# A two-block transformer layer on one core: first loads on one queue, one more product behind each modulation sum, attention outputs a slab earlier, the convolution's sums as single products

## The reference

```python
def first_block(x, ...):
    xn = rms_norm(x, norm1_g)
    (sg_u, sg_v, g_q, g_k, g_v, g_r, g_a, a_q, a_k, a_v, c_a, c_g) = split(xn @ w_in)
    y_a = spatial_gating(gelu(sg_u), gelu(sg_v), ...)        # layer norm over sg_v first
    y_b = gated_linear_attention(g_q, g_k, g_v, g_r, g_a, ...)
    y_c = band_chunk_attention(a_q, a_k, a_v, rel_bias)      # softmax(q k^T + bias) v, 8 heads of 64
    y_d = conformer_conv(c_a, c_g, ...)                      # depthwise conv, 31 taps, then layer norm
    merged = sum(sigmoid(xn @ w_gate[n] + b_gate[n]) * (y @ w_branch[n]) for n, y in ...)
    h = x + merged @ w_out
    h = h + square(relu(rms_norm(h) @ w_ff1)) @ w_ff2
    h = h + sigmoid(rms_norm(h) @ w_ple_gate + b) * (p @ w_ple)
    return rms_norm(h)

def second_block(x, c, ...):
    mod = silu(c) @ ada_w + ada_b                            # six vectors of 1,024: the modulation
    h = modulate(rms_norm(x), sh1, sc1)
    mq, mk, mv, mo, mi, mf, aq, ak, av, ga, gb = split(h @ w_in + b_in)
    ym = mlstm(...)                                          # 4 heads of 128
    ya = attention(rope(aq), rope(ak), av)                   # causal here, 8 heads of 64
    merged = sigmoid(ga) * (ym @ p_mlstm) + sigmoid(gb) * (ya @ p_moba)
    x = x + g1 * (merged @ w_out)
    h = modulate(rms_norm(x), sh2, sc2)
    x = x + g2 * ((silu(h @ w_gate) * (h @ w_up)) @ w_down)
    return rms_norm(x)
```

## Time and profile before

| what | before |
|---|---|
| three runs | 918.73, 921.71 and 918.3 us; median 918.73 |
| profiled execution | 917.34 us, of it 916.0 us span |
| PE busy | 897.2 us (98% of the span), 7,348 matmul records |
| DVE busy | 729.7 us (80%) |
| ACT busy | 569.7 us (62%) |
| GpSimd busy | 1.9 us |
| share of the chain that ended last | PE 86%, DVE 7%, ACT 4%, DMA 1%, issue 1% |
| DMA | 189.83 MB, mean 207 GB/s |

### The profile page before, as it was taken

How to read it: one execution, slowest core, us unless ns; L and a number is a source line. 1 busy time by engine, 2 the same in 40 slices (tenths; PEclk the granted TensorE clock), 3 DMA queues, 4 the chain that set the end, 5 groups by cost and what they waited for, 6 DMA issues and landing times.

```text
span 916.0 us, 18439 instructions
## 1 busy us (share of the span) xinstructions
PE 897.2 (98%) x7348; PEld 870.9 (95%) x7348; DVE 729.7 (80%) x1150; ACT 569.7 (62%) x828; POOL 1.9 (0%) x9
## 2 busy tenths in 40 slices
PE   8999999999999999999999989999999999999996
PEld 7999989999999999999999989988999999999996
DVE  5778998889997899888875989987789885555554
ACT  6848456676576687654445777667695664544542
POOL 0000000000000000000000000000000000000000
PEclk9999999999999999999999999999999999999998
DMA  8766546455875689988856546653536656666541
GB/s 302 250 189 220 156 142 202 156 169 194 290 252 176 226 306 341 346 315 306 326 167 202 183 155 201 208 165 119 173 123 197 188 171 201 189 194 197 186 160 47
DMA packets 53157, 189.83 MB, mean 207 GB/s; under 512 B 6208, under 2 KB 6736, under 8 KB 52944
## 3 DMA queue, kind: packets, MB, share of 16 engines
q1 hardware_dynamic: 52496, 187.60, 62.1%
q10 hardware_dynamic: 576, 1.05, 0.3%
HBM read 186.53 MB, written 1.05 MB: 205 GB/s over the span
## 4 chain that ended last, share of the span: by engine, by line
PE 86%; DVE 7%; ACT 4%; issue 1%; DMA 1%; ACTq 0%; DVEq 0%
PE bank L1003 25%; PE bank L1005 25%; PE bank L1006 25%; DVE wlo L1041 2%; PE bank L977 2%; PE bank L979 2%; PE bank L978 2%; ACT whi L1853 1%; DVE cv L1118 1%; DMA H<-in_xT 1%; PE bank L712 1%; DVE Alo L1076 1%; PE bank L949 1%; PE bank L952 0%; PE bank L956 0%
## 5 line engine op out<-in xcount | busy, mean ns | idle before, releaser
L1041 DVE TENSOR_TENSOR wlo<-raw,whi 128x1024 fp32r<-128x1024 f32 x297 | 360.4, 1220 | 110.2 <-ACT whi L1853 109.7
L1853 ACT ACTIVATE whi<-raw 128x1024 fp32r<-128x1024 f32 x297 | 312.1, 1057 | 200.3 <-PE bank L1006 185.9
L1003 PE MATMUL bank<-Alo,whi 128*128 128x256 f32 x1376 | 388.0, 282 | 2.5 <-ACT Ahi L1873 1.3
L1005 PE MATMUL bank<-Ahi,wlo 128*128 128x256 f32 x1376 | 382.8, 278 | 0.0
L1006 PE MATMUL bank<-Ahi,whi 128*128 128x256 f32 x1376 | 382.8, 278 | 0.0
L1003 PEld LDWEIGHTS bank<-Alo,whi 128*128 128x128 f32 x1376 | 259.4, 188 | 7.9 <-issue 5.5
L1006 PEld LDWEIGHTS bank<-Ahi,whi 128*128 128x128 f32 x1376 | 259.4, 189 | 0.0
L1005 PEld LDWEIGHTS bank<-Ahi,wlo 128*128 128x128 f32 x1376 | 258.7, 188 | 0.4 <-issue 0.2
L1005 PE MATMUL bank<-Fhi,wlo 128*128 128x256 f32 (+1 forms) x288 | 81.0, 281 | 0.0
L1006 PE MATMUL bank<-Fhi,whi 128*128 128x256 f32 (+1 forms) x288 | 81.0, 281 | 0.0
L1003 PE MATMUL bank<-Flo,whi 128*128 128x256 f32 x256 | 72.2, 282 | 0.0
(11 more groups left out here) (398 smaller groups left out, 1355.7 us busy)
## 6 DMA issues: line engine op xcount, KB each, us to landing
raw<-in_stream SPq DMA_DIRECT2D x298, 512.0 KB, 4.3
araw<-in_ada SPq DMA_DIRECT2D x48, 512.0 KB, 6.0
TB<-in_TB SPq DMA_DIRECT2D x1, 1536.0 KB, 7.0
a8r<-a SPq DMA_DIRECT2D x16, 64.0 KB, 2.9
bc<-in_bc SPq DMA_DIRECT2D x1, 896.0 KB, 6.1
out<-H SPq DMA_DIRECT2D x3, 256.0 KB, 2.2
H<-in_xT ACTq DMA_DIRECT2D x2, 256.0 KB, 6.9
H<-in_xT ACTq DMA_DIRECT2D x1, 512.0 KB, 9.6
```

The costliest lines, as they stand in the source:

```text
L1003: pe.matmul(os[j], wh, xl, start=k == 0 and (wide or j == 0), stop=False, skip_group_check=not wide)
L1005: pe.matmul(os[j], wl, xh, start=False, stop=False, skip_group_check=not wide)
L1041: v.tensor_tensor(wlo[:, s % NHL, :], raw[:, s % NRAW, :], whi[:, s % NHL, :].bitcast(F32), ALU.subtract).then_inc(*lo_v.up(s))
L1853: a.activation(whi[:, s % NHL, :], raw[:, s % NRAW, :], ACT.Copy).then_inc(*hi.up(s))
```

## The change

Five edits, all in the written-out order or in single instructions:

1. **First loads.** x is loaded by SP, between the first slabs, in three pieces of 1, 3 and 4 column tiles (ACT loaded 2, 2 and 4). The first columns of `cols` stay on ACT. `WARM` goes from 10 to 11.
2. **Modulation sums.** Behind each of the six groups of eight transposes stands one more product, ones times 256 columns of `mats`, in fp32, into bank 5, whose result nobody reads.
3. **Attention order.** In `att` and `att2` the outputs of a pair of heads come one slab earlier, and the scores of the next pair stand right behind them in the same slab. DVE makes the low part of an output ahead of the next pair's scores, ACT its high part ahead of the next exponentials.
4. **Gates.** The four sigmoids of `gab` become a task: two at slab 215, two at slab 217.
5. **Convolution sums.** DVE adds the two halves of what is to be summed once more (`added_up`, 128x256), and PE sums with one product in place of two, for mean and variance.

```diff
-    "att": ([44, 49, 50, 51, 55, 56, 57, 61, 62, 63, 67, 69],
-            [45, 47, 51, 52, 53, 57, 58, 59, 63, 64, 65, 70],
-            [45, 49, 51, 51, 55, 57, 57, 61, 63, 63, 67, 69]),
+    "att": ([n for h in range(4) for n in (44 + 6 * h, 49 + 6 * h, 50 + 6 * h)],
+            [n for h in range(4) for n in (45 + 6 * h, 47 + 6 * h, 51 + 6 * h)],
+            [n for h in range(4) for n in (45 + 6 * h, 49 + 6 * h, 50 + 6 * h)]),
...
+    "gates2": ([], [], [215, 217]),
...
-WARM = 10
+WARM = 11
+
+XTILES = (slice(0, 1), slice(1, 4), slice(4, 8))
...
-            for s in range(4):
-                load_slab(s)
+            for q, c in enumerate(XTILES):
+                sp.dma_start(H[:, c, :], A["xT"][:, c, :]).then_inc(*x_in[q].up("in", by=16))
+                load_slab(q)
+            load_slab(3)
...
-                    for j in range(2):
-                        i = pe.matmul(banks[3][:, 0:T], ones[:, :], scr[:, n * 512 + j * T:n * 512 + j * T + T],
-                                      start=j == 0, stop=j == 1)
-                    i.then_inc(*conv_pe.up(tag))
+                    pe.matmul(banks[3][:, 0:T], ones[:, :], scr[:, n * 512:n * 512 + T], start=True, stop=True
+                              ).then_inc(*conv_pe.up(tag))
...
                     i.then_inc(*ada_pe.up(cb))
+
+                    pe.matmul(banks[5][:, 0:T], ones[:, :], mats[:, 0:T], start=True, stop=True)
                     yield
...
+            def added_up(tag, x, y):
+                w.wait_ge(*conv_v.at("pairs", tag))
+                v.tensor_tensor(x, x, y, ALU.add).then_inc(*conv_v.up("sum", tag))
...
+            def gates2():
+                w.wait_ge(*drained_s.at("gab", 7))
+                for p in range(4):
+                    g = gab[:, 4 * p:4 * p + 4, :]
+                    a.activation(g, g, ACT.Sigmoid).then_inc(*gab_s.up(p))
+                    if p % 2:
+                        yield
...
-            for q, c in enumerate((slice(0, 2), slice(2, 4), slice(4, 8))):
-                a.dma_start(H[:, c, :], A["xT"][:, c, :]).then_inc(*x_in[q].up("in", by=16))
```

92 lines of the change are left out of this document (34 added, 58 removed), and 3 rows, old and new, of the table STEPS.

## The result

The changed kernel took 913.57 us (median of 22 runs, 911.1 to 920.37), the kernel before 919.14 (22 runs, 915.84 to 925.85); the ratio is 0.9939, 95% interval 0.992 to 0.9959, so about 5.6 us less. I had said 917.0, from 914.8 to 921.0, and gave 0.07 to a gain of over 0.5%. The gain is real, and over three times the 1.75 us of the sum.

A forecast was written before the change was run, and what follows sets the result against it. TensorE, busy 897.2 of 916.0 us, was taken as the bound. Start -4.2, convolution -0.9, extra products +2.6, attention order -0.5 + 1.25 sum to -1.75, from a median of 918.73 to 917.0 us, range 914.8 to 921.0.

The forecast's parts named there:

- Extra products: Modulation sums: six unread fp32 products at 0.43 us each, with no gap to cover them; +2.6 us, upper bound +2.9.
- no lower pace to be cured: Modulation sums: matmuls behind the transposes stay at 0.12 us, so a product there wins back no clock pace.
- Start: First loads: x lands earlier and v runs mostly at the fast pace; -4.2 us, from -2.5 to -4.4.
- Convolution: Convolution sums: two summing products fewer on TensorE, 0.43 us each; -0.9 us.
- the addition that I called hidden: Convolution: VectorE's new addition ends by 257.76 us, before TensorE comes at 257.95, so it costs nothing.
- Attention order: att and att2: five format changes saved, -0.5 us (0 to -1.0); outputs waiting for copies, +1.25 (0.7 to 2.2).
- the three places named: Slabs 50, 62 and 217: outputs wait for ScalarE's copies, 0.4, 0.4 and 0.45 us.
- Two things that I held at nothing: att2: low and high parts lengthen the chain ending in the 0.9 us wait, left at 0; shorter steps had no term.
- (1): Start: the loads don't come earlier and v starts only 0.5 us earlier; sum +0.8, 919.6 us; chance 0.12.
- (2): Start: the pace stays low through v; all 48 matmuls at it give +6.5, 925 us; chance 0.05.
- (3): Attention: copies late at all eight pairs, 3.2 us in place of 1.25; sum +0.2, 918.9 us; chance 0.10.
- (4): More gain: the upper ends together and the wait of 0.9 us gone; -3.9, 914.8 us; chance 0.06.

The follow-up runs named there:

- a2: The kernel before with the six extra products alone; 0.9958 of the kernel before, 914.5 us.
- a1: The changed kernel without the six extra products; 0.9992 of the kernel before, 917.14 us.
- a3: The kernel before with only the new first loads (x on SP between the slabs, eleven warm-up products); 0.9956 of the kernel before, 915.8 us.
- a4: The kernel before with only the new attention order and the gates' task; 1.0011 of the kernel before, 921.24 us.
- c3: The changed kernel with the three pieces of x issued by the ACT queue again; 917.12 us in one run.
- c4: The changed kernel with four warm-up products in place of eleven; 919.43 us in one run.
- b4: The kernel before with one more product at slab 237; 0.9994 of the kernel before, 917.32 us.
- b3: The changed kernel with one more product at slab 237; 0.9964 of the kernel before, 917.72 us.
- e1: The changed kernel with attention order and gates as before, and x in four pieces; 0.9931 of the kernel before, 911.37 us.
- d2: The changed kernel with attention order and gates as before; 0.9934 of the kernel before, 911.57 us.
- e2: Same as e1, with one more product over 64 rows behind slab 240; 0.995 of the kernel before, 913.22 us.

## Why the prediction was wrong

**Extra products: the step that failed.** The prediction said that "nothing covers it", took +2.6 us, and added "so there is no lower pace to be cured". The product's own price was right, 0.43 each. Wrong was that I took the step of slab matmuls for one number, 0.12 us, and read it at two decimals beside a single sum. The trace of before had both steps in it: the long one at 350 us (172 records where the changed kernel has 179), the short one at 740 (1,319 where it has 1,276). The six products change the step of five stretches, together 1,286 matmuls (1,286 x 4.4 ns = 5.7 us), and of what follows the last (0.5): some 6.1 us, less 2.2 for five products and 0.4 for the first, behind which a2 has the long step as before. Shown by taking them away (a1) and by adding them alone (a2): -3.9 instead of +2.6, an error of 6.5 us. The granted clock is 1.00 at either step, and twelve transposes do as well as a product; so the rule of the Trainium skill (TensorE: Matmul & The Clock Gate, part 4), which I had set aside, isn't what pays here either.

**Start: -4.2 forecast, -2.0 to -2.5 by the traces of a3 and the changed kernel against a2 and a4.** Queue, order and pace came as forecast (c3, c4). The sizes were off: the first half of slab 0 was cast at 5.64, and not at 4.91, where the first copy of x ended, since the slab stood behind x; and I had left out the second piece, 384 KB at 7.25, for which v waits 0.3 to 1.6 us. The 21.89 of the earlier trace rows, where v ends, was also one draw: a2 and a4, with the same start, are through 0.55 and 0.7 earlier.

**Convolution: -0.9 forecast, -0.67 by the starts.** The first sum gave its 0.43. The second got 0.28 longer, since TensorE waits for the addition that I called hidden. After, for the earlier trace rows:

```profile
252.90 0.69 DVE L1131 TENSOR_TENSOR scr<-ypad 128x512 f32<-128x512 f32 x1
253.62 0.43 DVE L1101 TENSOR_TENSOR scr<-scr 128x256 f32<-128x256 f32 x1
...
253.38 0.28 PE L999 MATMUL bank<-Ahi,whi 128*128 128x256 f32 x1
254.76 0.28 PE L998 MATMUL bank<-Ahi,wlo 128*128 128x256 f32 x1
```

Those two matmuls lie 1.38 us apart, for 1.10 before. The addition took 0.43 and not 0.68, but TensorE came 0.48 us behind the start of VectorE's first sum, where it had come 1.43 behind it. It had gained the 0.43 of the first sum and 0.52 in the stretch between the two, 120 matmuls, which now stands at the short step (13.38 us for 13.90). So the two products saved bring 0.15, and that stretch the other 0.52. All 15 profiles with edit 5 have this stretch at the short step, and all five without it (before, a2, a3, a4, b4) at the long. That step wasn't in the forecast.

**Attention order: -0.5 + 1.25 forecast, +0.4 in a4.** The waits for copies were there at the three places named, and at no others. They cost 2.3 us by the starts, not 1.25. The change of format saved more than I took: outputs and scores apart take 1.00 + 1.05 us, together 1.86 (2.10 less the slab's own 0.24), so 0.19 each, not 0.1. Two things that I held at nothing weren't: shorter steps in att (336 matmuls, 1.5 us), and longer waits in att2 (1.4 for 0.9, 0.6 for Ymlo). They nearly cancel.

**Rivals.** (1) and (2) did not happen: x landed at 0.74 + 3.5 = 4.2, and v ran at the higher pace from the start. (3) did not happen, though the copies' waits cost 2.3 us at three places. (4) had the sign and not the cause. Without the products the forecast was -4.35, and the terms measured for the rest come to -2.2 to -3.1: there I had expected too much, and that hid part of the 6.5 us missed at the products. With the measured terms, -2.3 (start) - 0.4 (att) + 0.3 to 1.2 (att2) - 0.7 (convolution and its step) + 0.4 (the first extra product) - 4.0 (sums two to six) = -5.8 to -6.7, against -5.6 measured.

**Still open.** What in the engine makes the two steps, and why a given piece leaves one or the other. That the last stretch's step makes the two clusters is argued and was not switched at will. The traces have 6.4 us between the two steps, and the clusters lie 6 apart. Among the kernels with many runs, the four profiles with the long step there lie in their kernel's upper cluster (after 917.0, a2 919.54, b3 919.28, e1 917.79) and the seven with the short one in the lower (before, a1, a3, a4, b4, d2, e2). The granted clock doesn't divide them: its mean lies between 0.992 and 0.998 in both clusters of the kernel before. It does mark a small third group there, seven runs of 919.1 to 920.1 us, all at 0.991. The kernels with edits 3 and 4 (after, a1, a4, b3) have 26 of 58 runs in the upper cluster, those with the new start or the extra products but the old order (a2, a3, d2, e1, e2) 7 of 60, but the kernel before itself has 36 of 120 over all rounds. The one direct test of the order, a4, has 6 of 12 beside 11 of 35, too few to tell whether an order so many slabs earlier acts on the last stretch.

## What to carry to other kernels

When TensorE is busy 98% of the time, its busy time isn't its work: count matmul records over long windows of every stage, and compare the step lengths, from start to start, before costing any edit by its instructions. A wait in a list may count from a modelled end, so price it by the starts as well. In this kernel a piece between two dense stretches had a second price or gain, the step that it left behind; with 240 matmuls behind it, 4.4 ns each outweighed a product of 0.43 us. If times of one kernel lie in two clusters, one profile is one draw: line up two traces event by event, and look where they part though the programs are the same.

## What was not expected of the hardware

- Two steps of fp32r matmuls of 256 columns at the same granted clock of 1.00, 113.3 and 117.8 ns, each held for up to 1,438 steps, with the long one costing up to 6.4 us of 915 in one stretch.
- The step behind a piece at one place can be the same in every case (short 65 times of 65 behind sums two to six with the product, long six times of six behind a product ahead of eight transposes), and yet no property tried here (kind, bank, length, signal) foretells it at another place. Behind a wait of 1.4 us it was short 8 times and long 12.
- The granted clock fell to half (0.54 over a window of 3.5 us) for 3.4 us behind sixteen small products (moving tiles of 64x64) in seven profiles of 20, whose code is the same there, 1.6 us each time.
